# A hybrid attention layer on one core: the sample group's attention outputs in a bank of their own, and the value products ahead of the turn of q and k

## The chip, the core and the metric

The program runs on one core of one Trainium2 chip. The metric is device time in microseconds of one execution; the median of three runs counts. PE (TensorE) multiplies, DVE (VectorE), ACT (ScalarE) and POOL (GpSimd) work elementwise, and SP issues most of the DMA. Each engine works through a list of its own; semaphores order the lists against each other.

## The reference, cut to what matters

One layer of a hybrid decoder is computed for a prompt of 1024 tokens and for a sample group of 8 sequences with 8 new tokens each. Attention heads and a convolution stand side by side, their outputs go through one output projection, and a gated feed-forward block follows.

```python
z = rms_norm(x) @ w_in                        # q | k | v | a | gate
q, k = rms_norm(q), rms_norm(k)               # 8 heads of 64
attn = dilated windows (128,1), (512,4), (2048,16), combined by their softmax denominators
c = silu(layer_norm(causal_depthwise(a * sigmoid(gate), 31 taps)))
x = x + concat(attn, c) @ w_out
x = x + (silu(h @ w_gate) * (h @ w_up)) @ w_down,   h = rms_norm(x)
```

The prompt group attends to itself, the sample group to a cache of 1024 positions and its own new tokens. New cache rows and convolution states are outputs too. All products are made in float32 by three products of split operands (high times high, high times low, low times high: lines 330 to 332).

## The kernel before, in words

The stages are: the projections of the convolution branch (to about 140 us); q, k and v of the first pair of heads (to about 160 us); the attention loop (about 163 to 541 us); the rest of the output projection; the feed-forward block (about 600 us to the end), which is nothing but products for PE.

**The attention loop** has 40 steps: 4 pairs of heads (`p`), 10 steps each (`s`, in `STEPS`). Steps 0 and 5 are the sample group's two halves of 4 sequences ("s"), the other eight the prompt's query blocks of 128 tokens ("p", block `i`). `n = 10 p + s`. The order on each engine is written out by hand in one loop per engine; nothing schedules it. In step n:

- PE makes `scores(n + 1)` (products of q and k, lines 739, 743, 753), in pairs 0 to 2 the q, k and v columns of one token tile of the next pair (`qkv`, 24 products, lines 330 to 332, tile z, into bank 7), `turn_probs(n)` (transposes of the probabilities, lines 765, 774, into banks 4 and 5), `turn` (transposes of the q and k made one step earlier, lines 718, 720, into bank 7 too, so it must wait until ACT has emptied the tile just made: semaphore `z_ev`), and `values(n - 1)` (products of probabilities and values, lines 792 for the sample group, 808 and 815 for the prompt).
- DVE makes `mask_min` (mask and row minimum out of PSUM, line 1337), two or three `tap`s of the convolution (line 1249; each is one instruction over 1024 columns and one over the sample group's 64, both read SBUF twice), `normalise` (lines 1346, 1351), `square_sum` (lines 1312, 1315) and copies out the attention outputs: `block_outputs` (four prompt blocks of bank 6, line 1360), `scale_sample` (line 1389, into `so`) and `sample_outputs` (line 1360 over 64x32).
- ACT makes `exps` (line 1086), `keep` (empties the q, k, v tile: lines 1040, 1044, 1053), `copy_probs` (line 1095), `evict` (the turned q and k, lines 1079, 1081), and the high parts of the next weights (`high`, line 982).
- POOL makes the low parts of the weights (`low`, line 518, three per pair, around step 0) and the scaling of q and k (lines 534, 537, 543).

**The sample group's outputs** take a longer way. The products of step 0 or 5 are summed by `values`, scaled by DVE into `so`, turned back by PE (`turn_sample`, line 822) into the same bank, and copied out by DVE. Before, `sample_bank(p, half)` names the second score bank of the other parity: it is free from the end of `mask_min(n + 1)` until `scores` of the step after next. So PE makes these values early in steps 1 and 6 (before `qkv`), turns them at the end of the same step, and `scores` for steps 3 and 8, which PE issues in steps 2 and 7, wait for `d_se`, that is for `sample_outputs`, with which DVE begins steps 2 and 7. The prompt's outputs have bank 6.

In the last pair no q, k, v is left to make; there pieces of the output projection and of the convolution's layer norm (`fill`, `take_fill`) stand in three places of each step from step 3 on.

## Time and profile before

| | |
|---|---|
| median of three runs | 1425.53 us (1424.42 to 1427.17) |
| the profiled execution, its time | 1423.0 us |
| its span, first to last instruction | 1420.9 us |
| PE busy / PE weight loads busy | 93% / 88% of the span |
| DVE, ACT, POOL busy | 47%, 22%, 33% |
| mean granted clock of TensorE | 0.974 |
| chain that ended last | PE 82%, DVE 10%, issue 2%, ACT 2%, POOL 2% |

Times in the rows are in microseconds from the start of the span, durations of one instruction of a group in nanoseconds. In a timeline, a row is a run of like instructions: its start, its length, engine, line, operation, output and inputs, how many, and in brackets how long the engine sat idle before it and what ended that. Matmuls are pipelined, so the length of a run of them has a tail over which the next has already begun; the distance between two starts is the time that the first takes on PE. A TensorE clock of 1.0 is 2.4 GHz and 0.5 is 1.2 GHz.

### The profile page before, as it was taken

How to read it: one execution, taken by the hardware profiler on the slowest of the kernel's cores; microseconds unless marked ns; L12 is line 12 of the kernel's file. 1: busy time of each engine (PE TensorE's matmuls, PEld its weight loads, DVE VectorE, ACT ScalarE, POOL GpSimd, SP SyncE). 2: the span in 40 equal slices, each digit the busy share in tenths (PEclk: the TensorE clock that was granted, in tenths of full speed). 3: DMA queues.
4: the chain of work that ended last, by engine and by line, in shares of the span. 5: the costliest groups of instructions: out<-in, count | busy, mean ns of one | idle time of the engine just before them, and what ended most of it. 6: DMA issues, size and time to landing. Idle time of an engine off the chain costs nothing.

```text
span 1420.9 us, 22561 instructions
## 1 busy us (share of the span) xinstructions
PE 1317.1 (93%) x9084; PEld 1253.3 (88%) x9084; DVE 667.1 (47%) x1227; ACT 314.3 (22%) x715; POOL 474.0 (33%) x307
## 2 busy tenths in 40 slices
PE   6999789799795869999999999999999999999998
PEld 6999667677674559999999999999999999999998
DVE  6697867767678445583141414131313131313234
ACT  6212434444344325342101010101000000000000
POOL 0232522424215322533624242424242424333220
PEclk9999999999897879999999999999999999999999
DMA  7214143332435201038511410141114111411103
GB/s 223 64 53 145 31 150 101 111 104 77 138 104 213 83 18 43 31 119 282 194 44 60 149 60 31 52 157 46 45 45 163 44 47 35 171 33 60 38 0 126
DMA packets 50693, 131.07 MB, mean 92 GB/s; under 512 B 14480, under 2 KB 26640, under 8 KB 50064
## 3 DMA queue, kind: packets, MB, share of 16 engines
q1 hardware_dynamic: 45088, 95.47, 20.1%
q10 hardware_dynamic: 5504, 34.11, 7.1%
q8 instruction: 81, 1.33, 0.4%
q14 instruction: 20, 0.16, 0.0%
HBM read 120.09 MB, written 43.28 MB: 115 GB/s over the span
## 4 chain that ended last, share of the span: by engine, by line
PE 82%; DVE 10%; issue 2%; ACT 2%; POOL 2%; DMA 1%; SPq 0%; ACTq 0%; DVEq 0%; POOLq 0%
PE ps L330 25%; PE ps L332 25%; PE ps L331 25%; DVE uc L1249 5%; PE ps L743 1%; PE ps L808 1%; PE ps L739 1%; PE ps L815 1%; DVE ml_c L1494 1%; POOL zst L537 1%; PE ps L849 1%; PE ps L753 1%; DMA out_nk_p<-zst 1%; DVE tb L1337 1%; PE ps L718 1%
## 5 line engine op out<-in xcount | busy, mean ns | idle before, releaser
L637 POOL TENSOR_TENSOR wf<-raw,small 128x1024 fp32r<-128x1024 f32 x60 | 113.9, 1898 | 433.2 <-PE ps L332 423.4
L1573 DVE TENSOR_TENSOR pr<-ps,sg 128x362 f32<-128x362 f32 (+1 forms) x66 | 35.4, 536 | 411.0 <-ACT sg L1209 411.0
L330 PE MATMUL ps<-mh_a,wf 128*128 128x362 f32 (+1 forms) x624 | 207.7, 333 | 14.0 <-DVEq L1442 3.7
L1249 DVE SCALAR_TENSOR_TENSOR uc<-uc,small 128x1024 f32<-128x1024 f32 x240 | 215.1, 958 | 0.1
L332 PE MATMUL ps<-mh_a,wf 128*128 128x362 f32 (+1 forms) x624 | 205.5, 329 | 0.0
L331 PE MATMUL ps<-ml_a,wf 128*128 128x362 f32 (+1 forms) x624 | 205.4, 329 | 0.0
L331 PE MATMUL ps<-ml_c,wf 128*128 128x362 f32 (+1 forms) x624 | 203.9, 327 | 0.0
L332 PE MATMUL ps<-mh_c,wf 128*128 128x362 f32 (+1 forms) x624 | 203.9, 327 | 0.0
L330 PE MATMUL ps<-mh_c,wf 128*128 128x362 f32 (+1 forms) x624 | 203.5, 326 | 0.0
L1591 DVE TENSOR_TENSOR y<-ps,y 128x362 f32<-128x362 f32 (+1 forms) x264 | 139.4, 534 | 107.9 <-PE ps L332 107.9
L332 PE MATMUL ps<-ah,wf 128*128 128x364 f32 (+1 forms) x528 | 174.0, 330 | 0.0
L331 PE MATMUL ps<-al,wf 128*128 128x364 f32 (+1 forms) x528 | 173.7, 329 | 0.0
L330 PE MATMUL ps<-ah,wf 128*128 128x364 f32 (+1 forms) x528 | 173.4, 328 | 0.0
L1209 ACT ACTIVATE sg<-ps 128x362 f32<-128x362 f32 (+1 forms) x66 | 31.3, 474 | 620.7 <-PE ps L332 620.6
L639 POOL TENSOR_TENSOR wf<-raw,wf 128x1024 fp32r<-128x1024 f32 x60 | 147.5, 2458 | 4.7
L330 PEld LDWEIGHTS ps<-mh_a,wf 128*128 128x128 f32 x624 | 117.8, 189 | 18.3 <-DVEq L1442 4.3
L332 PEld LDWEIGHTS ps<-mh_a,wf 128*128 128x128 f32 x624 | 118.2, 189 | 0.0
L331 PEld LDWEIGHTS ps<-ml_a,wf 128*128 128x128 f32 x624 | 117.8, 189 | 0.2
L330 PEld LDWEIGHTS ps<-mh_c,wf 128*128 128x128 f32 x624 | 117.4, 188 | 0.0
L331 PEld LDWEIGHTS ps<-ml_c,wf 128*128 128x128 f32 x624 | 117.3, 188 | 0.0
L332 PEld LDWEIGHTS ps<-mh_c,wf 128*128 128x128 f32 x624 | 117.2, 188 | 0.0
L330 PE MATMUL ps<-wq,xh 128*128 128x384 f32 x288 | 103.4, 359 | 3.7 <-POOL wq L518 2.6
(150 smaller groups left out, 2118.7 us busy)
## 6 DMA issues: line engine op xcount, KB each, us to landing
raw<-in_w_stream SPq DMA_DIRECT2D x94, 512.0 KB, 3.5
skt<-in_kT_c SPq DMA_DIRECT2D x32, 384.0 KB, 5.3
sv<-in_v_c SPq DMA_DIRECT2D x32, 384.0 KB, 6.8
xr<-in_xT SPq DMA_DIRECT2D x8, 544.0 KB, 4.3
out_yT<-y SPq DMA_DIRECT2D x8, 544.0 KB, 2.7
y<-in_xT SPq DMA_DIRECT2D x1, 3264.0 KB, 15.3
out_nv_p<-vn SPq DMA_DIRECT2D x32, 64.0 KB, 1.8
out_nk_p<-zst SPq DMA_DIRECT2D x32, 64.0 KB, 1.6
```

What stands on the lines that cost most here:

```text
L330: e.matmul(out, wh, mh_, start=first, stop=False)
L331: e.matmul(out, wh, ml_, start=False, stop=False)
L332: return e.matmul(out, wl, mh_, start=False, stop=last)
L537: pool.tensor_tensor(rows, rows, r.unsqueeze(2).broadcast_to([P, 4, DH]), ALU.mult).then_inc(z_n, 1)
L637: pool.tensor_tensor(hi(m), src, zeros, ALU.add).then_inc(w_hi, 1)
L639: pool.tensor_tensor(lo(m), src, hi(m).bitcast(F32), ALU.subtract).then_inc(w_lo, 1)
L718: pe.transpose(turned(j), zst[:, z % 2, cols], ident[:]).then_inc(z_tr, 1)
L739: pe.matmul(ps[32 * r:32 * r + 32, (b + h) * 512:(b + h) * 512 + nf], q_[hr[h], i * P + 32 * r:i * P + 32 * r + 32], keys[:, r, :], start= ...
L1209: act.activation(sg[:, k6 % 2, 0:bn], bank(2 * (k6 % 2), bn), ACT.Silu).then_inc(gu_si, 1)
L1249: dve.scalar_tensor_tensor(out=dst, in0=src, scalar=w, in1=dst, op0=ALU.mult, op1=ALU.add).then_inc(s, 1)
L1573: dve.tensor_tensor(pr[:, k6 % 2, 0:bn], bank(2 * (k6 % 2) + 1, bn), sg[:, k6 % 2, 0:bn], ALU.mult).then_inc(gu_pr, 1)
L1591: dve.tensor_tensor(y[:, oc, b0:b0 + bn], bank(4 + m % 4, bn), y[:, oc, b0:b0 + bn], ALU.add).then_inc(dn_y, 1)
```

## The change

Three things change. The sample group's outputs move to columns 0 to 127 of bank 6, which they share in time with the prompt's: `values` of a sample step waits until the prompt's last four blocks are copied out (`d_oe`), `values` of blocks 0 and 4 until the sample group's are (`d_se`), and the waits on `d_tt` in the sample's `values` and on `d_se` in `scores` go. Its transposition back moves from the end of steps 1 and 6 to steps 2 and 7, after the scores and before `qkv`; `scale_sample` moves to the start of steps 2 and 7 on DVE, `sample_outputs` behind `mask_min`, and `block_outputs` ahead of it. In every step PE makes `values(n - 1)` before `turn`, and in steps 1 and 6 after `qkv` instead of before it. The reciprocal of the sample's denominators gets a column of its own (`rden_s`), since it is read one step later.

```diff
--- before.py
+++ after.py
@@ -160,6 +160,7 @@
         rs8 = small[:, 59:68]
         mns, den, rden = small[:, 68:72], small[:, 72:76], small[:, 76:80]
         ssz = small[:, 80:84]
+        rden_s = small[:, 209:210]
 
         def place(at, name, shape, dt=F32):
 
@@ -251,9 +252,8 @@
 
             return bank(7, w, j * P)
 
-        def sample_bank(p, half):
-
-            return bank(2 * ((NSTEP * p + 5 * half + 1) % 2) + 1, P)
+
+        sample_bank = bank(6, P)
 
         g_in, c_in = sem("gain_in"), sem("consts_in")
         x_in = [sem(f"x_in{k}") for k in range(KT)]
@@ -728,8 +728,6 @@
                 q_, k_ = qt[p % 2], kt_[p % 2]
                 if kind == "p":
                     pe.wait_ge(t_ev, 2 * (NT * p + i + 2))
-                    if s in (3, 8):
-                        pe.wait_ge(d_se, 2 * p + s // 5 + 1)
                     nf = far(i)
                     k0 = max(i - 1, 0) * P
                     hr = [slice(DH * h, DH * h + DH) for h in range(2)]
@@ -780,9 +778,10 @@
                 kind, i = STEPS[s]
                 pe.wait_ge(d_ev, 2 * n + 2)
                 if kind == "s":
-                    pe.wait_ge(d_tt, ROWS0[n + 2])
+                    if 2 * p + i:
+                        pe.wait_ge(d_oe, 2 * p + i)
                     r = slice(64 + NEW * i, 64 + NEW * (i + 1))
-                    out = sample_bank(p, i)
+                    out = sample_bank
                     for c in range(CKT + 1):
                         for bb in range(4):
                             if c == 0:
@@ -795,7 +794,7 @@
                     last.then_inc(d_pv, 1)
                     return
                 if i % 4 == 0:
-                    pe.wait_ge(d_oe, 2 * p + i // 4)
+                    pe.wait_ge(d_se, 2 * p + i // 4 + 1)
                 if i == 2:
                     pe.wait_ge(d_vf, 32 * (p + 1))
                 first = max(i - 1, 0)
@@ -819,7 +818,7 @@
 
             def turn_sample(p, half):
                 pe.wait_ge(d_so, 2 * p + half + 1)
-                pe.transpose(sample_bank(p, half), so[:], ident[:]).then_inc(d_ot, 1)
+                pe.transpose(sample_bank, so[:], ident[:]).then_inc(d_ot, 1)
 
             def project(out, ks, oc, g):
                 b0, bn = BLOCKS[g]
@@ -873,21 +872,19 @@
                 fills = p == NPAIR - 1 and s in FILL
                 if n + 1 < NALL:
                     scores(n + 1)
-                if s in (1, 6):
-                    values(n - 1)
+                if s in (2, 7):
+                    turn_sample(p, s // 5)
                 if z_at(p, s) is not None:
                     qkv(z_at(p, s))
                 if fills:
                     fill(s, 0)
                 turn_probs(n)
-                if s in (1, 6):
-                    turn_sample(p, s // 5)
+                if fills:
+                    fill(s, 1)
+                if n >= 1:
+                    values(n - 1)
                 if turn_at(p, s) is not None:
                     turn(turn_at(p, s))
-                if fills:
-                    fill(s, 1)
-                if n >= 1 and s not in (1, 6):
-                    values(n - 1)
                 if fills:
                     fill(s, 2)
             values(NALL - 1)
@@ -1343,7 +1340,7 @@
                 dve.wait_ge(d_ex, ROWS0[n + 1])
                 r = 2 * (n % 2)
                 k = len(heads(n))
-                dve.reciprocal(rden[:, r:r + k], den[:, r:r + k]).then_inc(d_rc, 1)
+                dve.reciprocal(rden_s if k == 1 else rden[:, r:r + k], den[:, r:r + k]).then_inc(d_rc, 1)
                 if k == 1:
                     return
                 dve.wait_ge(d_rc, n + 1)
@@ -1386,11 +1383,11 @@
                 n = NSTEP * p + 5 * half
                 dve.wait_ge(d_pv, n + 1)
                 dve.wait_ge(d_rc, n + 1)
-                dve.tensor_scalar(so[:], sample_bank(p, half), col(rden, n, 0), None, ALU.mult).then_inc(d_so, 1)
+                dve.tensor_scalar(so[:], sample_bank, rden_s, None, ALU.mult).then_inc(d_so, 1)
 
             def sample_outputs(p, half):
                 dve.wait_ge(d_ot, 2 * p + half + 1)
-                o = sample_bank(p, half).rearrange("p (b c) -> p b c", c=32)
+                o = sample_bank.rearrange("p (b c) -> p b c", c=32)
                 c0 = SEQ + NEW * half
 
                 def part(a, r):
@@ -1462,15 +1459,15 @@
                 p, s = divmod(n, NSTEP)
                 fills = p == NPAIR - 1 and s in FILL
                 if s in (2, 7):
-                    sample_outputs(p, s // 5)
-                if n + 1 < NALL:
-                    mask_min(n + 1)
-                if s in (1, 6):
                     scale_sample(p, s // 5)
                 if s == 6:
                     block_outputs(2 * p)
                 if s == 1 and p >= 1:
                     block_outputs(2 * p - 1)
+                if n + 1 < NALL:
+                    mask_min(n + 1)
+                if s in (2, 7):
+                    sample_outputs(p, s // 5)
                 if s == 5 and p < NPAIR - 1:
                     fill_qb(p + 1)
                 for _ in range(TAPS_STEP.get(n, 0)):
```

**How the lists of instructions move.** First PE, step 3 of the first pair, from the second head's transposed probabilities on (`tb` probabilities, `zst` q and k before the turn, `pt` turned probabilities, `vn` values). Before:

```order
L774 MATMUL ps<-ident,tb 128x128 [waits probs_out,normed]
L774 MATMUL ps<-ident,tb 128x128
L774 MATMUL ps<-ident,tb 32x128
L718 MATMUL ps<-ident,zst 128x128 [waits qkv_evicted,qk_turned_out,qkv_normed]
L718 MATMUL ps<-ident,zst 128x128
L808 MATMUL ps<-pt,vn0 64x128 [waits probs_out]
L808 MATMUL ps<-pt,vn0 64x128 x3
L753 MATMUL ps<-skt,qb 32x512 [waits qb_ready,sample_k_in0,qk_turned_out,scores_masked]
```

Changed:

```order
L772 MATMUL ps<-ident,tb 128x128 [waits probs_out,normed]
L772 MATMUL ps<-ident,tb 128x128
L772 MATMUL ps<-ident,tb 32x128
L807 MATMUL ps<-pt,vn0 64x128 [waits probs_out]
L807 MATMUL ps<-pt,vn0 64x128 x3
L718 MATMUL ps<-ident,zst 128x128 [waits qkv_evicted,qk_turned_out,qkv_normed]
L718 MATMUL ps<-ident,zst 128x128
L751 MATMUL ps<-skt,qb 32x512 [waits qb_ready,sample_k_in0,qk_turned_out,scores_masked]
```

The two transposes of q and k with their waits stand behind the value products instead of ahead of them; no row is added.

Second, PE, from the end of `turn_probs` of step 6 of the first pair to the scores of step 7 (`so` the scaled sample outputs). Before:

```order
L774 MATMUL ps<-ident,tb 128x128 [waits probs_out,normed]
L774 MATMUL ps<-ident,tb 128x128
L774 MATMUL ps<-ident,tb 96x128
L822 MATMUL ps<-ident,so 128x128 [waits sample_scaled]
L718 MATMUL ps<-ident,zst 128x128 [waits qkv_evicted,qk_turned_out,qkv_normed]
L718 MATMUL ps<-ident,zst 128x128
L739 MATMUL ps<-kt0,qt0 32x160 [waits sample_out,qk_turned_out,scores_masked]
L739 MATMUL ps<-kt0,qt0 32x160 x7
L743 MATMUL ps<-kt0,qt0 128x256 x2
```

Changed (from the middle of the sample's value products, which now stand here, to the transposition back):

```order
L791 MATMUL ps<-sv,pt 32x128 [waits sample_v_in3]
L791 MATMUL ps<-sv,pt 32x128 x20
L791 MATMUL ps<-vfar,pt 32x128 x4
L718 MATMUL ps<-ident,zst 128x128 [waits qkv_evicted,qk_turned_out,qkv_normed]
L718 MATMUL ps<-ident,zst 128x128
L737 MATMUL ps<-kt0,qt0 32x160 [waits qk_turned_out,scores_masked]
L737 MATMUL ps<-kt0,qt0 32x160 x7
L741 MATMUL ps<-kt0,qt0 128x256 x2
L821 MATMUL ps<-ident,so 128x128 [waits sample_scaled]
```

The wait on `sample_out` at the scores is gone; the transposition back, with its wait on `sample_scaled`, now stands behind them, with the next tile's `qkv` right behind it.

Third, DVE, from the masks of step 1 of the second pair to those of step 2 (`mkp` mask; ISA is the masking instruction). Before:

```order
L1337 ISA small 128x1
L1389 TENSOR_SCALAR so<-ps,small 128x128 [waits den_recip,values_summed]
L1360 COPY ao<-ps 128x4x4x32 [waits values_summed]
L1249 SCALAR_TENSOR_TENSOR uc<-uc,small 128x1024 [waits conv_prompt]
L1249 SCALAR_TENSOR_TENSOR uc<-uc,small 128x8x8 [waits conv_samples]
...
L1315 TENSOR_SCALAR small<-small 128x4 [waits qkv_square_sums]
L1360 COPY ao<-ps 64x32 [waits sample_turned]
L1360 COPY ao<-ps 64x32
L1337 ISA tb,small<-ps,mkp 128x288 [waits probs_turned,scores]
```

Changed:

```order
L1348 TENSOR_SCALAR tb<-tb,small 128x128
L1357 COPY ao<-ps 128x4x4x32 [waits values_summed]
L1334 ISA tb,small<-ps,mkp 128x256 [waits probs_turned,scores]
...
L1312 TENSOR_SCALAR small<-small 128x4 [waits qkv_square_sums]
L1386 TENSOR_SCALAR so<-ps,small 128x128 [waits den_recip,values_summed]
L1334 ISA tb,small<-ps,mkp 128x288 [waits probs_turned,scores]
L1334 ISA small 128x1
L1334 ISA tb,small<-ps,mkp 128x288
L1334 ISA small 128x1
L1357 COPY ao<-ps 64x32 [waits sample_turned]
```

The big copy out of bank 6 now comes ahead of the step's masks, the scaling has moved past three taps, the normalising and the squares to the start of step 2, and the two small copies behind the masks of step 2.

## Rows read from the trace of the kernel before

**Rows 1.** The page's 40 slices: busy tenths of PE.

```profile
PE   6999789799795869999999999999999999999998
```

**Rows 2.** Waits of PE, 165 to 545 us: sum, times, longest.

```profile
PE ps L739 <- DVE ao L1360: 19.4, 5, 6.2
PE ps L718 <- ACT vn L1053: 11.1, 21, 0.6
PE ps L739 <- DVE ml_a L1368: 8.4, 2, 6.9
...
PE ps L720 <- ACT vn L1053: 2.5, 3, 0.8
```

**Rows 3.** Timeline of PE, first pair, steps 2 and 4.

```profile
193.76 0.31 PE L720 MATMUL ps<-ident,zst 64*128 64x64 f32 x2 [0.84 <-ACT vn L1053]
...
207.77 0.82 PE L774 MATMUL ps<-ident,tb 128*128 128x128 f32 x6
209.22 0.41 PE L718 MATMUL ps<-ident,zst 128*128 128x128 f32 x2 [0.62 <-ACT vn L1053]
209.55 0.66 PE L808 MATMUL ps<-pt,vn 128*64 128x128 f32 x8
210.14 0.65 PE L815 MATMUL ps<-pt,vfar 32*64 32x32 f32 x16
210.73 0.55 PE L739 MATMUL ps<-kt,qt 64*32 64x96 f32 x16
```

**Rows 4.** Timeline of ACT, step 4 of the first pair.

```profile
209.96 0.39 ACT L1081 ACTIVATE kt<-ps,small 128x128 f32<-128x128 f32 x1
```

**Rows 5.** Timeline of PE, steps 6 and 7, first pair; last row second pair.

```profile
219.05 0.66 PE L739 MATMUL ps<-kt,qt 64*32 64x128 f32 x16
...
220.28 1.52 PE L792 MATMUL ps<-sv,pt 128*32 128x128 f32 x48
...
226.35 0.82 PE L774 MATMUL ps<-ident,tb 128*128 128x128 f32 x6
227.00 0.27 PE L822 MATMUL ps<-ident,so 128*128 128x128 f32 x1
...
229.01 0.78 PE L739 MATMUL ps<-kt,qt 64*32 64x160 f32 x16 [0.81 <-ACT kt L1081]
...
317.53 0.79 PE L739 MATMUL ps<-kt,qt 64*32 64x160 f32 x16 [1.25 <-DVE ao L1360]
```

**Rows 6.** Windows of qkv: stretch, length, PE busy (count), granted clock, DMA share, GB/s.

```profile
318.98:324.69 5.71, 5.71 (x26) 0.72 0.08 23
364.85:371.44 6.59, 6.59 (x27) 0.61 0.00 0
...
230.42:234.62 4.20, 4.20 (x25) 1.00 0.10 31
```

**Rows 7.** Timeline of PE, step 9 of the first pair: the turn, next scores.

```profile
253.16 0.41 PE L718 MATMUL ps<-ident,zst 128*128 128x128 f32 x2 [0.40 <-ACT vn L1053]
...
255.11 0.49 PE L743 MATMUL ps<-kt,qt 64*128 64x128 f32 x4
```

**Rows 8.** Timeline of all engines, step 0 of the second pair.

```profile
258.90 2.39 DVE L1249 SCALAR_TENSOR_TENSOR uc<-uc,small 128x64 f32<-128x64 f32 x1
...
261.59 3.35 POOL L518 TENSOR_TENSOR wq<-raw,wq 128x1024 fp32r<-128x1024 f32 x1
```

**Rows 9.** Timeline of DVE, second pair, the end of the work before step 2's masks.

```profile
272.79 0.38 DVE L1360 COPY ao<-ps 64x32 f32<-64x32 f32 x2
```

**Rows 10.** Timeline of PE, step 2 of the second pair.

```profile
273.32 0.36 PE L739 MATMUL ps<-kt,qt 64*32 64x32 f32 x16 [6.16 <-DVE ao L1360]
...
274.77 0.69 PE L330 MATMUL ps<-wq,xh 128*128 128x384 f32 x1
```

**Rows 11.** Timeline of PE, last pair, steps 7 and 8.

```profile
510.01 0.80 PE L739 MATMUL ps<-kt,qt 64*32 64x160 f32 x16 [1.44 <-DVE ml_a L1368]
...
521.30 1.29 PE L853 MATMUL ps<-ones_c,sq 128*128 128x1 f32 x6 [3.40 <-POOL sq L584]
```

## The prediction

> **What bounds the kernel now.** I read the page first. PE is busy in nine tenths of nearly every slice; the gaps are in slices 4 to 16, the attention loop [rows 1]. After it nothing but products follows, and the change does not touch them. So I asked for PE's waits between 165 and 545 us. Two kinds can be touched by the change: scores of steps 2 and 7 that wait for the copy of the sample group's outputs (19.4 + 8.4 = 27.8 us in 7 waits, up to 6.9 us each), and the turn of q and k, which waits for ACT to empty the tile just made (11.1 + 2.5 = 13.6 us in 24 waits) [rows 2]. The timelines of PE, ACT, DVE and POOL around single steps then show what would end each wait next. The reader should see in them that PE sets the pace of steps 2 to 9, while DVE and POOL set it at steps 0 and 1.
>
> **Term 1, the turn behind the value products.** In step 4, PE's transposed probabilities start at 207.77 and take 0.65 (226.35 to 227.00, the same six of them [rows 5]), so PE is free at 208.42; the turn starts at 209.22, takes 0.33, and the value products take 1.18 (209.55 to 210.73) [rows 3]. In the new order the value products run from 208.42 to 209.60, the emptying is over by then, and the turn follows at once: the step is 0.80 shorter. In step 2 the value products last only some 0.37, less than the wait of 0.84 [rows 3], so 0.36 is saved and the rest of the wait stays. By the same working steps 3, 5, 7 and 8 save 0.59, 0.65, 0.79 and 0.58. That is 3.8 a pair, in three pairs **11.3**. From below, the listed idle times alone would give 3.2 a pair, 9.5. What could take the gain back is the next `qkv`, which waits for the turned q and k to be evicted: they were evicted 1.13 after the start of the turn (209.22 to 209.96 + 0.39) [rows 3, 4]. The turn takes 0.33 and the first part of the scores 0.55 [rows 3], the second part comes on top, so the eviction stays hidden, with little room. I cost it at nothing; without that cover a step would lose about half a microsecond.
>
> **Term 2, steps 6 and 7.** From the scores issued in step 6 (219.05) to the q, k, v products of step 7 (230.42, a window's start) were 11.37 [rows 5, 6]. In the new order this path is: scores 1.23 (to 220.28); value products of the sample group and q, k, v products together 6.07 (220.28 to 226.35, in either order); transposes 0.65; turn 0.33; scores 1.41 (229.01 to 230.42); transposition back 0.20. Sum 9.9, gain 1.5. In the two other pairs the scores waited 1.25 instead of 0.81 [rows 5], so about 1.9 each. Together **5.4**. The new wait in it is that of the transposition back for the scaling. DVE had finished the work of step 6 just before 229.01, the sample copies of 0.38 included, and the wait for the sample's products in the middle of it (0.8) goes; so the scaled outputs lie ready near 227.6, a microsecond before PE asks. Nothing is queued too late behind it.
>
> **Term 3, the clock after that wait.** In the second pair the 24 products of step 7 took 5.71 at a granted clock of 0.72, in the first pair 4.20 at 1.00 [rows 6]. Without the wait ahead of them I take the full clock: **1.5**. From below nothing.
>
> **Term 4, steps 0 to 2 of each pair.** Here DVE is late. POOL's three splits of the next weights stand around step 0, and DVE's taps and they shut each other out: the tap over 64 columns took 2.39 and ended with the split beside it [rows 8]. After the third split (261.59 + 3.35 = 264.94) DVE worked without a stop until 273.17 (272.79 + 0.38) [rows 8, 9]; only then came the scores at 273.32, and the q, k, v products at 274.77 [rows 10]. In the new order the scores (1.45) are made meanwhile, and the small copies (0.38) come later; the transposition back (0.20) stands between the scaling and the q, k, v products. That is 1.6 earlier. But the splits start later: in step 9 the turn moves behind the value products of 1.6 (253.16 to 255.11, less 0.33) [rows 7], thus from 253.16 to 254.26; ACT evicts it and only then makes the high parts that the splits need. ACT's queue was 0.35 late anyhow, so 0.75 remains. Net 0.85 at the second and third pair, 1.6 at the first, where no step 9 comes before, and in the last, where the small copies are four instructions and POOL splits the mixed outputs as well, I take 1.0: with **4.4** in all. The sample's value products (1.8), which in step 1 move behind the q, k, v products, cost nothing as long as DVE is later still: they end near 269, the scaling near 273.5. From above, all of the 0.75 would be hidden and 6.4 gained; from below nothing.
>
> On the port, the Trainium skill (SBUF — State Buffer, section "SBUF: two separate sides") says that whichever of DVE and GpSimd starts first holds the shared ports for its whole instruction and that the other blocks fully. The trace agrees with the blocking (2.39 for 64 columns). By that rule the first tap of step 0, which now starts before the first split, would hold the split up by what is left of it, and term 4 would be some 0.8 smaller over the pairs.
>
> **Term 5, the last pair's second half.** The scores of step 7 waited 1.44 for the sample copies [rows 11], and the value products of 1.8 stood ahead of the layer norm's pieces, with DVE waiting for them. After those scores the chain runs over the masks, the exponentials, ACT's high part, POOL's split and POOL's sums of squares to the products at 521.30, which waited 3.40 for POOL [rows 11]. So what the scores gain is passed on. Between nothing and 1.44 + 1.8 = 3.2 I take **2.3**, since the block copy and the pieces of the layer norm keep DVE busy for the rest.
>
> The sum is 11.3 + 5.4 + 1.5 + 4.4 + 2.3 = 24.9. Against the profiled execution's 1423.0 that is 1398.1; the median of the runs is 2.5 higher, so the forecast for the median is **1400.6**.
>
> **The rivals.**
>
> *A, the clock comes back at the pairs' starts too.* PE's gap in steps 1 and 2 shrinks from 6.16 [rows 10] to some 3.5, broken by value products and scores. After the long gap the third pair's products of step 2 took 6.59 at 0.61, against 4.20 at 1.00 [rows 6]. If they ran at the full clock, up to 2.4 more would be won there, and near 4.7 over three pairs: 1396. Against it stands that a short gap was enough to lower the clock to 0.72 in Term 3, and that the products of step 1 wait for weights before it. The Trainium skill (TensorE: Matmul & The Clock Gate, "What's actually happening") calls the low clock the default state, which activity lifts; by that rule a denser PE would come out nearer to this case. Chance 0.14.
>
> *B, the eviction is the next wait.* ACT's queue is keep, probabilities, eviction; if the eviction comes late in most steps, q, k, v products wait for it and Term 1 is given back. The room is only the second part of the scores [rows 3, 4]. The time would be 1400.6 + 11.3 = 1412. Chance 0.08.
>
> *C, the sample wait only moves.* The transposition back now stands ahead of q, k and v. If DVE brought the scaling as late as it brought the copies, Terms 2 to 5 would shrink to the scores' own length or less; with Term 1 alone left, 1414. For it: at the pairs' starts it does move so. Against it: in the second halves DVE has the microsecond of Term 2. Chance 0.08.
>
> *D, slower: the splits slide into step 1.* Should the third split come more than 2 us later than before, it would meet the three taps of step 1 instead of DVE's PSUM work, and each of the six tap instructions can be shut out; three stalls of 2.39 [rows 8] at three pair starts cost 21.5, and the longer gaps keep the low clock for all of step 2's products, up to 2.4 each [rows 6], 7.2 in all. Term 4 goes, and 28.7 stands against the 20.5 that is left: 8 slower, 1434. I work out 0.75 and not 2, so the chance is 0.02.
>
> That the change does not do what it says I hold for unlikely: the lists show the rows moved and no wait added besides those named.
>
> **How the numbers follow.** The forecast has 0.62, A 0.14, B 0.08, C 0.08, D 0.02; 0.06 lies between forecast and no change. The range of 8 in 10 reaches from A with a little (1395) to the sum of the lower bounds, 9.5 + 5.4 = 14.9 without Terms 3 to 5, which is 1410.6: 1395 to 1410. Under 0.2% (2.9 us) a measurement of this kernel can't tell from no change. Faster by more: forecast, A, B, C and most of the rest, 0.95; within it 0.03; slower 0.02.
>
> **What would show it.** In the changed profile the turn should wait only in step 2 (about 0.5) and hardly elsewhere; the scores of steps 2 and 7 should wait for nothing; the transposition back should wait some 3 us at three or four pair starts and not in the second halves; step 7's products of the second pair should take 4.2; the stretch after the loop should be as long as before. The prediction is wrong if `qkv` waits for ACT in most steps, if the transposition back waits in steps 7, or if taps in step 1 run beside a split.

## The result and the profile after

The changed kernel takes **1392.26 us** (median of 4 runs, 1389.53 to 1395.79) against 1425.11 of the kernel before: ratio 0.9769, 95% interval 0.9738 to 0.9799. The direction is as forecast. The size is not: 1392.3 lies below the forecast of 1400.6 and below the low end of the range, 1395. The profiled execution took 1394.82, its span 1392.9, at a mean granted clock of 0.975 (before 0.974).

The page's slices of the changed kernel answer to [rows 1]; PEclk is the granted clock in tenths.

```profile
PE   6999799899995799999999999999999999999998
...
PEclk9999899899997989999999999999999999999999
```

In slices 6, 11 and 15, which had 8, 7 and 6, PE is now at 9; the start of the loop (slice 5), that of the second pair (slice 8, now 8) and that of the last pair (slices 13 and 14) are left. The list of PE's waits, 160 to 545 us of the changed kernel, answers to [rows 2] (sum, times, longest):

```profile
PE ps L821 <- DVE so L1386: 8.9, 4, 2.8
PE ps L772 <- DVE tb L1348: 8.5, 2, 6.6
...
PE ps L330 <- ACT kt L1078: 3.6, 2, 1.8
...
PE ps L720 <- ACT vn L1050: 1.4, 3, 0.5
```

Of the 27.8 us at the scores nothing is left, and of the turn's 13.6 us only the three waits of 0.5 in step 2. The new wait is that of the transposition back (L821), at the four pair starts alone. The timeline of PE, first pair, steps 4 and 6 to 7, answers to [rows 3, 5]:

```profile
205.89 0.82 PE L772 MATMUL ps<-ident,tb 128*128 128x128 f32 x6
206.64 0.66 PE L807 MATMUL ps<-pt,vn 128*64 128x128 f32 x8
207.23 0.65 PE L814 MATMUL ps<-pt,vfar 32*64 32x32 f32 x16
207.81 0.44 PE L718 MATMUL ps<-ident,zst 128*128 128x128 f32 x2
208.18 0.55 PE L737 MATMUL ps<-kt,qt 64*32 64x96 f32 x16
...
215.97 0.66 PE L737 MATMUL ps<-kt,qt 64*32 64x128 f32 x16
...
224.38 0.78 PE L737 MATMUL ps<-kt,qt 64*32 64x160 f32 x16
...
225.72 0.33 PE L821 MATMUL ps<-ident,so 128*128 128x128 f32 x1
```

No row has a bracket: value products, turn, scores and transposition back follow each other without a wait. From step 6's scores to step 7's q, k, v products (a window's start, 225.80) are 9.83 us; the prediction worked out 9.9.

To see where the time went I cut the attention loop at four kinds of points of PE's timeline: start of step 2's q, k, v products, end of step 9's, first product of the layer norm, end of the loop.

| stretch, in us | before | after | less |
|---|---|---|---|
| loop's start to step 2's products, first pair | 27.06 | 25.30 | 1.76 |
| step 9's end to step 2's products, second / third pair | 23.05 / 23.06 | 21.23 / 21.17 | 1.82 / 1.89 |
| step 9's end to the first layer norm product, last pair | 31.99 | 30.25 | 1.74 |
| step 2's 24 products, three pairs | 5.08, 5.63, 6.59 | 4.24, 6.97, 4.24 | 1.85 |
| from their end to step 9's end, three pairs | 59.40, 61.39, 59.86 | 54.66, 54.67, 54.67 | 16.65 |
| from there to the loop's end, last pair | 78.56 | 74.70 | 3.86 |
| loop | 381.67 | 352.10 | 29.57 |

The loop began 1.67 later in this execution (161.85 against 160.18), ahead of anything that the change touches, and what follows it is as long as before (879.05 against 878.95 us).

### The profile page after: what moved, and what is told of

The parts are those of the page before. It is cut to its first block, busy times and chain, and to the rows that moved or that the text cites. A ratio compares the mean times of both kernels' runs of the same rounds, so it can differ in the third digit from the quotient of the medians.

```text
span 1392.9 us, 22561 instructions
## 1 busy us (share of the span) xinstructions
PE 1319.2 (95%) x9084; PEld 1255.7 (90%) x9084; DVE 669.7 (48%) x1227; ACT 316.7 (23%) x715; POOL 473.1 (34%) x307
## 4 chain that ended last, share of the span: by engine, by line
PE 85%; DVE 9%; issue 2%; POOL 2%; DMA 1%; ACT 1%; SPq 0%; ACTq 0%; DVEq 0%; POOLq 0%
PE ps L330 26%; PE ps L332 25%; PE ps L331 25%; DVE uc L1246 4%; PE ps L772 1%; PE ps L807 1%; PE ps L814 1%; PE ps L741 1%; DVE ml_c L1491 1%; POOL zst L537 1%; PE ps L848 1%; PE ps L751 1%; PE ps L737 1%; DMA out_nk_p<-zst 1%; DVE tb L1334 1%
## 5 line engine op out<-in xcount | busy, mean ns | idle before, releaser
L1246 DVE SCALAR_TENSOR_TENSOR uc<-uc,small 128x1024 f32<-128x1024 f32 x240 | 210.7, 940 | 0.3
```

The source lines that it names most:

```text
L1246: dve.scalar_tensor_tensor(out=dst, in0=src, scalar=w, in1=dst, op0=ALU.mult, op1=ALU.add).then_inc(s, 1)
```

## The experiments

**The same kernel again.** No edit, six more executions.

> The changed kernel once more, unaltered. Its four runs fell into two pairs, 1394.8 and 1395.8, and 1389.7 and 1389.5, with mean granted clocks of 0.975 and 0.979; the profiled one was of the first kind, and in it the q, k, v products of step 2 of the second pair took 6.97 us at a clock of 0.57, those of the first and third pair 4.24 at 1.00. Clock theory: the two kinds differ in which products run at 1.2 GHz and in nothing else; more runs will lie at about 1389.6 or about 1395, and if the profile is of the faster kind, the products of step 2 take about 4.2 in all three pairs. Rival (the kinds differ in waits, as in how DVE and POOL come to share their port): the products' times are alike and the waits of PE differ by 5 us.

1395.13 us (median of 6, 1392.28 to 1404.36), ratio 0.9797, 0.9774 to 0.9820. The six do not gather at 1389.6 and 1395, and the profiled one (1392.28) is of neither kind. All ten executions of the changed kernel have the median 1394.7. The windows of step 2's products in this trace (stretch, length, busy time of PE, PEld, DVE, ACT and POOL, granted clock, DMA share, GB/s), and the turn back ahead of each:

```profile
185.66:189.90 4.24, 4.24 (x26) 4.21 (x26) 4.16 (x12) 1.15 (x4) 1.30 (x2) 1.00 0.67 234
265.71:271.52 5.81, 5.81 (x25) 5.78 (x26) 4.71 (x13) 1.15 (x4) 1.29 (x2) 0.71 0.69 225
347.37:353.18 5.81, 5.81 (x26) 5.78 (x27) 4.72 (x13) 1.15 (x4) 1.29 (x2) 0.71 0.48 171
```

```profile
185.56 0.33 PE L821 MATMUL ps<-ident,so 128*128 128x128 f32 x1 [2.32 <-DVE so L1386]
...
265.62 0.33 PE L821 MATMUL ps<-ident,so 128*128 128x128 f32 x1 [1.25 <-DVE so L1386]
...
347.27 0.33 PE L821 MATMUL ps<-ident,so 128*128 128x128 f32 x1 [2.21 <-DVE so L1386]
```

The same 24 products took 4.24, 5.81 and 5.81 here and 4.24, 6.97 and 4.24 above. The length of the wait does not decide it: 2.8 us was followed by either clock in one and the same execution, and 1.2 by either in the two. Every other stretch agrees within 0.5 us, except that step 1's products ran at other speeds (5.33, 6.89 and 7.04 us against 6.43, 6.45 and 6.42), and the wait behind them was longer or shorter by about as much. The two loops are equally long (352.11 and 352.10 us), so the 2.7 us between the two spans lie outside the loop: 1.5 ahead of it and 1.2 behind it. The two say nothing for or against the clock theory.

**The order alone.** The kernel before, with values ahead of the turn:

```diff
-                if turn_at(p, s) is not None:
-                    turn(turn_at(p, s))
                 if fills:
                     fill(s, 1)
                 if n >= 1 and s not in (1, 6):
                     values(n - 1)
+                if turn_at(p, s) is not None:
+                    turn(turn_at(p, s))
```

> The kernel before, with only the value products put ahead of the turn of q and k (in steps other than 1 and 6, where they already are). Terms as measured in the changed trace: about 3.3 us a pair from steps 2, 3, 4, 5, 7, 8 and 0.4 from step 9, in all 11, and perhaps 1.5 where the clock no longer falls in step 7. Forecast 1412 to 1415 against 1425.1. If the turn's place mattered for the pair starts as well (POOL's splits later, taps first), the waits of the scores of steps 2 shrink or grow by up to 1 us each. If the parts only work together, it is above 1418.

1412.42 us (1411.35 to 1414.59), ratio 0.9905, 0.9890 to 0.9919. From step 2's products to step 9's end, those products left out, it saves 3.27, 3.28 and 3.28 us: Term 1 by itself, 3.3 a pair and not 3.8. The waits for ACT at the turn (L718) are gone from its list, those at the scores stand:

```profile
PE ps L739 <- DVE ao L1360: 17.2, 5, 5.8
PE ps L739 <- DVE ml_a L1368: 8.4, 2, 6.9
```

**The bank alone.** The changed kernel with the turn ahead of the values again (the same edit backwards).

> The changed kernel, with the turn put back ahead of the value products in every step: the sample group's bank, its turn one step later and the order on DVE stay. Additive theory: it gives back the 11 us of the reordering and keeps the rest: 1403 to 1406. Rival (the bank is worth little, since the wait only moves to the scaling): 1412 or more. In steps 7 no wait of the scores on DVE; in steps 2 a wait for the scaling of 1 to 3 us.

1409.01 us (1404.91 to 1412.32), ratio 0.9883, 0.9865 to 0.9902: a few us above what I had expected. In its trace all three of step 2's products had the low clock (5.81, 5.80, 5.81), and the turn's waits are back (L718, 11.4 us in 21). The pair starts are as short as in the changed kernel (25.30, 21.31, 21.33 us), so nearly the whole of Term 4 belongs to the bank (the order alone has 26.46, 22.91 and 22.88, that is 0.6, 0.1 and 0.2 less than before). Between the pair starts it saves 0.8, 2.8 and 1.3 us. With the 3.3 of the order that leaves 0.6 of each pair to the two together, since in step 6 the value products now stand between the emptying and the turn. The medians fit: the order alone saves 12.9, the bank alone 16.3, both together 30.7 by the ten executions.

**The turn's place in step 9.** The changed kernel, but in step 9 alone the turn ahead of the values:

```diff
+                if s == 9 and turn_at(p, s) is not None:
+                    turn(turn_at(p, s))
                 if fills:
                     fill(s, 1)
                 if n >= 1:
                     values(n - 1)
-                if turn_at(p, s) is not None:
+                if s != 9 and turn_at(p, s) is not None:
```

> The changed kernel, with the turn ahead of the value products in step 9 alone, so that ACT can make the high parts of the weights as early as before. My step in term 4: the splits on POOL start 0.75 later because of the turn; undone, the three pair starts would win 0.75 each, less the 0.4 that step 9 loses: about 1 us faster in all. Rival, from the changed trace: the third split ended only 0.26 us later than before, since the first tap now runs ahead of the first split and POOL waits for one tap less; then the turn's place costs nothing there and this kernel is 1 to 2 us slower.

1395.18 us (1390.67 to 1402.49), ratio 0.9795, 0.9768 to 0.9822. The pair starts took 21.31 us, against 21.23 and 21.17. Turning earlier brings nothing, so the 0.75 us that I took off Term 4 for it does not exist. Where it went is seen in the timeline of DVE and POOL, second pair, changed kernel:

```profile
249.96 7.32 DVE L1246 SCALAR_TENSOR_TENSOR uc<-uc,small 128x1024 f32<-128x1024 f32 x4
250.75 5.05 POOL L518 TENSOR_TENSOR wq<-raw,wq 128x1024 fp32r<-128x1024 f32 x2 [1.15 <-ACT wq L979]
...
257.16 2.37 POOL L518 TENSOR_TENSOR wq<-raw,wq 128x1024 fp32r<-128x1024 f32 x1
...
257.39 2.42 DVE L1348 TENSOR_SCALAR tb<-tb,small 128x128 f32<-128x128 f32 x2
259.73 1.06 DVE L1357 COPY ao<-ps 128x512 f32<-128x512 f32 x1
```

```profile
246.05 1.03 PE L772 MATMUL ps<-ident,tb 128*128 128x128 f32 x8
...
248.63 0.44 PE L718 MATMUL ps<-ident,zst 128*128 128x128 f32 x2
```

The turn does come later, 2.58 after the transposes of step 9 (246.05 to 248.63) against 1.44 (251.72 to 253.16 in the trace before): the 1.1 that was worked out. But the third split ended 13.48 after those transposes (259.53) against 13.22 before (264.94 less 251.72), so only 0.26 later. The first tap now comes before the first split; the two taps with what shuts them out took 7.32 instead of 8.95, and the taps were over (257.28) when the third split had hardly begun (257.16), where before the last of them stood shut out until that split had ended [rows 8, 9]. So DVE's two normalising instructions, 0.48 us by themselves, now stand beside the third split (2.42) and no longer behind it. With the turn early in step 9 the order of before comes back: the first split begins at 249.52, ahead of the first tap (250.06), the taps take 8.93, and though the third split ends 13.19 after the transposes instead of 13.48, DVE begins its block copy 13.78 after them instead of 13.68. Of the splits' late start nothing reached DVE's end.

**The turn back behind q, k and v.** Would the last wait go? The changed kernel with `turn_sample` behind `qkv` on PE and `sample_outputs` behind the taps on DVE:

```diff
-                if s in (2, 7):
-                    turn_sample(p, s // 5)
                 if z_at(p, s) is not None:
                     qkv(z_at(p, s))
+                if s in (2, 7):
+                    turn_sample(p, s // 5)
```

> The changed kernel, with the sample's transposition back behind the q, k, v products of steps 2 and 7, and the small copies on DVE behind the taps. PE then has nothing to wait for before those products. If the wait for the scaling (8.9 us in 4 waits in the changed trace) is what is left of the old one, it goes: 6 to 9 us faster than the changed kernel, and the products after it come at the full clock more often. Rival (DVE sets the pace at the pair starts, whatever PE waits on): the scores of step 3 or the transposes of step 2 wait in its place and less than 3 us is won.

1394.37 us (1387.91 to 1399.13), ratio 0.9751, 0.9712 to 0.9790: nothing gained where 6 to 9 us were expected. Timeline of PE in the second pair, and the windows of the products of steps 2 and 3:

```profile
265.29 0.27 PE L821 MATMUL ps<-ident,so 128*128 128x128 f32 x1
...
268.22 0.69 PE L807 MATMUL ps<-pt,vn 128*64 128x128 f32 x4 [2.22 <-DVE ao L1357]
```

```profile
261.03:265.29 4.26, 4.26 (x26) 4.23 (x25) 4.19 (x13) 1.01 (x4) 1.52 (x2) 1.00 1.05 336
270.79:276.97 6.18, 6.18 (x26) 6.15 (x25) 5.85 (x13) 1.20 (x4) 0.89 (x2) 0.66 0.58 192
```

The pair starts are 3 us shorter (18.20 and 18.19), but the value products of block 0, which take bank 6 over, wait 2.2 for the copies (2.5 in the third pair), and behind this wait the clock is low in step 3 (6.18 and 6.06 where the changed kernel has 4.28; in the first pair, where the wait is 0.40, it is 4.27). The wait changes its place and takes the low clock along. Over the three pairs that comes out even. The profiled execution, the slowest of the four, loses another 7.5 us in the last pair, 4.1 of them by step 6's scores, where a split on POOL met DVE's normalising (Term 5 below). Whether that is the edit's doing one trace can't show.

**PE kept busy in the wait.** Ahead of `turn_sample` in step 2, twelve more products of 128x384 into the bank of q, k and v:

```diff
+                if s == 2 and z_at(p, s) is not None:
+                    pe.wait_ge(z_ev, z_at(p, s))
+                    for _ in range(12):
+                        pe.matmul(zbank, xh[:, 0, 0:P], wq[:, 0, 0:384], start=True, stop=True)
                 if s in (2, 7):
                     turn_sample(p, s // 5)
```

> The changed kernel, with 12 products more than the computation needs (384 columns each, into bank 7, overwritten by the q, k, v products that follow) ahead of the transposition back in step 2 of the first three pairs, where PE waits for DVE. They add nothing to the path where the wait is over 2.1 us (at 2.4 GHz), and about 1 us at the first pair, whose wait is 1.2. Clock theory: the products behind them take 4.2 us in all three pairs instead of 4.2 to 7.0, so the runs gather at the low end, about 1390 to 1392, with less spread. Rival (the clock there is set by what came further back, in step 1): the products still take 5.8 in some pairs, and the kernel is 0 to 2 us slower than the changed one.

1391.61 us (1388.46 to 1394.71), ratio 0.9746, 0.9712 to 0.9779. Windows of the needed products of step 2, and the turn back of the second pair:

```profile
187.73:191.97 4.24, 4.24 (x26) 4.20 (x25) 3.88 (x9) 0.32 (x2) 0.30 (x1) 1.00 0.79 277
267.82:272.06 4.24, 4.24 (x26) 4.21 (x27) 4.16 (x12) 1.15 (x4) 1.28 (x2) 1.00 0.65 246
347.93:352.17 4.24, 4.24 (x26) 4.21 (x26) 4.16 (x12) 1.15 (x4) 1.28 (x2) 1.00 0.69 252
```

```profile
267.72 0.33 PE L821 MATMUL ps<-ident,so 128*128 128x128 f32 x1 [0.54 <-DVE so L1390]
```

The added 2.35 us of products a pair cost nothing where DVE is waited for long enough (from step 1's to step 2's products 12.43 and 12.45 in the second and third pair, against 12.47 and 12.41 in the changed kernel) and 1.1 in the first pair (11.91 against 10.84), and all three stretches behind them ran at 1.00. Step 1's products were as slow as ever (6.68, 6.44 and 7.03), so the rival that it is they that set the clock of step 2 fell. The median is 3.1 below that of the ten executions. That fits (ten of fifteen at the low clock, 1.6 or more each, is some 3.2 for three pairs), but the runs overlap and their spread is no smaller than that of the first four (both 6.3 us), so the trace carries this reading and not the median.

**The block copy's place.** The changed kernel with `block_outputs` behind `mask_min` again, as before the change.

> The changed kernel, with only the order of two pieces on DVE put back: the copy of the prompt's four blocks behind the masks of steps 1 and 6 instead of ahead of them. The sample's value products wait for that copy. I expect next to nothing in the first three pairs (under 0.5 us each way), since at those steps PE makes q, k and v first, which covers 0.7 us; in the last pair's step 6 the multiplies of the layer norm come no earlier either. Within 1.5 us of the changed kernel. If the copy's place were part of why the pair starts gained more than I forecast, e9 to step 2 would be over 21.7 us instead of 21.2.

1395.72 us (1392.56 to 1399.06), ratio 0.9783, 0.9752 to 0.9815. The pair starts are 25.29, 21.17 and 21.17 us, the same to a tenth: at the pair starts this part of the change is worth nothing either way. In the last pair's step 6 it is worth something, against the expectation: PE waits 4.01 us instead of 3.24 for the multiplies of the layer norm, and step 7's scores come 0.6 later than in the trace of the turn in step 9, whose last pair is otherwise the same (45.00 against 44.36 after the first layer norm product). Step 2's products took 4.24, 4.24 and 5.81.

**Taps away from the pair starts.** If DVE is late there because of its taps, they should stand elsewhere. The same 24 a pair:

```diff
-TAPS_STEP = {n: 3 if n % NSTEP in (1, 3, 6, 8) else 2 for n in range((NPAIR - 1) * NSTEP)} | {30: 2, 31: 2, 32: 2}
+TAPS_STEP = {n: (1, 2, 2, 3, 3, 3, 3, 2, 3, 2)[n % NSTEP] for n in range((NPAIR - 1) * NSTEP)} | {30: 2, 31: 2, 32: 2}
```

> The changed kernel, with one tap fewer in each of steps 0 and 1 and one more in steps 3 to 5, 6 as before, so that DVE has 2.8 us less to do where PE waits for it. If the pair starts are bound by DVE's list behind POOL's third split, the wait for the scaling shrinks by about 1.4 us a pair (the tap of step 1; that of step 0 is hidden beside the splits anyhow), and PE's steps 2 to 9 hide the taps: 3 to 6 us faster in all. Rival (steps 3 to 5 have become bound by DVE since the reordering shortened them): the gain is given back there and the kernel is within 2 us or slower.

**1382.17 us** (1377.60 to 1382.22), ratio 0.9670, 0.9638 to 0.9702, faster than both kernels. Timelines of PE and DVE, second pair, and the window of step 2's products:

```profile
262.01 0.33 PE L821 MATMUL ps<-ident,so 128*128 128x128 f32 x1
```

```profile
261.25 0.35 DVE L1386 TENSOR_SCALAR so<-ps,small 128x128 f32<-128x128 f32 x1
```

```profile
262.09:266.35 4.26, 4.26 (x26) 4.23 (x27) 4.14 (x12) 1.15 (x4) 0.74 (x2) 1.00 1.04 305
```

The scaled outputs are there 0.4 before PE turns them back. The pair starts fell from 21.2 to 17.4 us, that is the wait of 2.8 and, with step 1's products at 5.5 instead of 6.4, another 0.9. Steps 3 to 9, which took the taps in, are as long as before to a hundredth (54.67, 54.66, 54.66 us).

**Further, once more, in the last pair, and in the old kernel.** The last four ran side by side on one chip; each is described in its expectation.

> The changed kernel with the taps of pairs 0 to 2 shared out as (0,1,2,3,3,3,3,3,3,3) over steps 0 to 9, one less in steps 0 and 1 than where they were (1,2,2,3,3,3,3,2,3,2). Theory (DVE's lateness at the pair starts is what the kernel pays for, and with (1,2,2,...) it is already paid off in pairs 0 to 2: PE had no wait for DVE there from 170 to 400 us): no further gain, 1380 to 1384 us, from the step-9 products to the step-2 products 17.3 as before. Rival one (the low clock in steps 0 and 1 comes from splits that DVE holds up): the splits end some 1 us earlier, 3 us in all, 1378. Rival two (three taps in seven steps are too many for DVE): waits of the transposes for `tb` appear in steps 5 to 9 and the time rises to 1386 or more.

1380.22 us (1379.08 to 1383.92), ratio 0.9677, 0.9651 to 0.9703: no further gain, as the first theory had it. Pair starts 17.38 and 16.98.

> The kernel with taps (1,2,2,3,3,3,3,2,3,2) once more, so that it stands beside the two above on one chip: 1379 to 1384 us. By the theory of the clock (a wait of 2.8 us ahead of step 2's products lowers it in some executions, none where there is no wait) the products of step 2 take 4.24 to 4.3 us in all of pairs 0 to 2 again. If the full clock in the first profile of it was luck, one or more of the three takes 5.8 or more.

1380.52 us (1379.04 to 1382.73), ratio 0.9679, 0.9655 to 0.9704. Step 2's products 4.24, 4.25 and 4.25. So the full clock was not luck.

> The changed kernel with 25 taps in each of pairs 0 to 2, as (1,2,2,3,3,3,3,3,3,2), and 0, 1 and 2 instead of 2, 2 and 2 at the start of the last pair. Theory (DVE's lateness again: in the last pair the transposes waited 6.6 and 2.0 us for the normalised probabilities, the turn back 2.7 and the first layer norm products 2.9 for the taps): most of these 14 us goes, against 1382 us I expect 1370 to 1375. Rival (POOL's splits and ACT set the start of the last pair, so that the waits only change their name): 1379 to 1383.

**1373.58 us** (1369.96 to 1376.36), ratio 0.9623, 0.9598 to 0.9649, the best of all, 6.9 below the kernel with the taps moved in three pairs. Timeline of PE at the start of the last pair, first that kernel, then this one:

```profile
407.36 0.48 PE L772 MATMUL ps<-ident,tb 128*128 128x128 f32 x1 [6.58 <-DVE tb L1348]
409.82 0.48 PE L772 MATMUL ps<-ident,tb 128*128 128x128 f32 x1 [1.99 <-DVE tb L1348]
...
417.44 0.47 PE L821 MATMUL ps<-ident,so 128*128 128x128 f32 x1 [1.79 <-DVE so L1386]
```

```profile
402.68 0.30 PE L772 MATMUL ps<-ident,tb 128*128 128x128 f32 x1 [0.94 <-ACT pt L1092]
404.28 0.47 PE L772 MATMUL ps<-ident,tb 128*128 128x128 f32 x1 [1.31 <-DVE tb L1348]
...
413.51 0.47 PE L821 MATMUL ps<-ident,so 128*128 128x128 f32 x1 [3.38 <-DVE so L1386]
```

The transposes' 8.6 us shrank to 2.3, the turn back gave 1.6 of it back. From step 9's end to the first layer norm product it is 4.9 less. The profiled execution of this kernel was the slowest of its six; what the medians show beyond 4.9 I can't place.

> The kernel before, with nothing changed but the taps: (1,2,2,3,3,3,3,2,3,2) over steps 0 to 9 of pairs 0 to 2. If the gain of moving taps and the gain of the change are independent (the change shortens what stands behind DVE at a pair start, the taps make DVE less late), the time falls as far as it did in the changed kernel, 12 to 13 us: 1411 to 1415, and the idle time of PE ahead of step 2's scores from 6.2 to about 2. If instead what holds those scores is the length of the way values, scaling, turn back, copies and not DVE's lateness, the gap stays over 4 and the time falls by less than 6: 1419 or more.

1414.86 us (1413.23 to 1417.62), ratio 0.9921, 0.9895 to 0.9947. The time is that of the first theory, the gap is that of the second: PE's timeline in the second pair has

```profile
267.33 0.36 PE L739 MATMUL ps<-kt,qt 64*32 64x32 f32 x16 [4.18 <-DVE ao L1360]
```

so 4.2 us are left of 6.2 [rows 10], and step 2's products behind it still took 6.15 and 5.78 us (4.26 in the first pair, behind a wait of 1.28). Moving taps saves 2.9 us at the second and third pair start in the old order and 3.85 in the new one, so the two gains are not independent there. In the old order the scores still wait for copies that stand behind step 1's taps and its normalising on DVE.

## Why the prediction was right or wrong

**What bounds the kernel**, and what would show it: right in all five points, but for one length. The turn waits in step 2 alone (0.5), the scores of steps 2 and 7 wait for nothing, the transposition back waits at four pair starts (1.2 to 2.8, not "some 3") and in no second half, step 7's products of the second pair took 4.25, and the stretch after the loop is as long as before.

**Term 1** (11.3) was mis-sized a little: alone it measured 9.8, 3.28 a pair. What was too low is the 0.65 for the six transposes. I took it from a place where a transposition back followed [rows 5]; with value products behind them they held PE for 0.75 (205.89 to 206.64), and the turn with scores behind it 0.37 instead of 0.33. The rest is as worked out: the eviction stayed hidden, `qkv` waits for ACT (L1078) only in step 1, so rival B fell.

**Terms 2 and 3** (5.4 and 1.5): right, but for a slip (1.5 + 1.9 + 1.9 is 5.3). With Term 1 they came to 16.65, so 6.8 for the two together; of it 0.6 a pair needs both parts of the change.

**Term 4** (4.4) is **the step that failed**. It measured 7.2: 1.76, 1.82, 1.89 and 1.74 at the four pair starts. (Its own parts, 0.85 twice, 1.6 and 1.0, are 4.3.) The 1.6 worked out from the scores, the copies and the turn back was right in the first pair. What was wrong was "0.75 remains" for the later splits, at the second and third pair. The prediction passed a delay of POOL's start on to DVE's end as if the two worked in a chain. They take turns instead, and which comes first changes what each is shut out by: the third split ended 0.26 later, and DVE did its normalising beside it instead of behind it. Turning early in step 9 put the old order of the two back and brought nothing (21.31 against 21.2). "From above, all of the 0.75 would be hidden and 6.4 gained" was the case that came. Why the last pair gave 1.74 and not the 1.0 taken for it, no run shows.

By the Trainium skill (SBUF — State Buffer, section "SBUF: two separate sides") of a DVE instruction with two SBUF inputs and a GpSimd instruction the one that starts first keeps the shared ports for its whole length. I had drawn from it that Term 4 would be smaller. The trace agrees with the blocking (two taps took 7.32 us beside the splits and 2.87 in step 9), not with that inference: an earlier tap cost the splits 0.26 us and spared DVE more.

**Term 5** (2.3) was too small: 3.9 in this trace. Step 7's scores came 3.9 earlier after the first layer norm product (42.81 against 46.72 us):

```profile
482.06 0.79 PE L737 MATMUL ps<-kt,qt 64*32 64x160 f32 x16
...
492.77 0.78 PE L852 MATMUL ps<-ones_c,sq 128*128 128x1 f32 x6 [1.02 <-POOL sq L584]
```

That looks like the whole of 1.44 + 1.8, but 1.5 of it was there before the sample group had a part in it, at step 6's scores (31.40 against 32.88 us). Of that 0.3 is how fast the first layer norm products ran (7.22 against 7.56 to the next products), and 1.2 is a wait of PE for DVE in step 3 that is gone. Timelines of DVE, POOL and PE there, before:

```profile
471.07 2.80 DVE L1351 TENSOR_SCALAR tb<-tb,small 128x320 f32<-128x320 f32 x2
471.21 4.90 POOL L518 TENSOR_TENSOR wf<-raw,wf 128x1024 fp32r<-128x1024 f32 x2 [8.16 <-ACT wf L982]
...
474.37 0.43 PE L330 MATMUL ps<-mh_a,wf 128*128 128x362 f32 x1 [1.16 <-DVE y L1412]
```

and changed:

```profile
446.70 0.68 DVE L1348 TENSOR_SCALAR tb<-tb,small 128x320 f32<-128x320 f32 x2
448.62 4.71 POOL L518 TENSOR_TENSOR wf<-raw,wf 128x1024 fp32r<-128x1024 f32 x2 [9.60 <-ACT wf L979]
```

In the trace before, the split begins while DVE normalises, and in the changed one it begins later. Whether they meet changes from one execution to the next: the two traces of the kernel with the taps moved have 0.68 and 2.81, and the stretch from the first layer norm product to the loop's end took 72.67 and 74.62 us in them. The trace of the turn in step 9, whose last pair is that of the changed kernel, has 2.81 as the one before. In it the scores of step 7 come 2.4 earlier (44.36), near the 2.3, of which 0.6 is the block copy's place; and from there to the loop's end 1.2 more is gained (30.59 against 31.84), which the prediction put at nothing when it took what the scores gain as simply passed on. In all that is 3.6 (74.95 against 78.56).

**Rival A, the clock at the pair starts,** came in part. The gap fell to 2.8, and to 1.2 in the first pair, not to 3.5. In five traces with this wait (the changed kernel twice, the bank alone, the turn in step 9, the block copy's place) the products behind it ran at full clock 5 times in 15 and took 5.80 to 6.97 the other ten. In the five traces where PE had at most a third of a microsecond to wait there (turn back late, taps moved twice, further, last pair) it was 15 of 15 at 4.24 to 4.28, and 3 of 3 with PE kept busy. So the wait causes the low clock, but not each time. The forecast had put these products at nothing; in the profiled execution they gave 1.9 (17.30 to 15.45 us for the three). That this is also part of why executions differ (the changed kernel spread from 1389.5 to 1404.4, the one with the taps moved from 1377.6 to 1382.7) is likely, but no two traces show it. I had given the two outcomes as one or the other, where each pair start draws anew. Rivals C and D fell: no wait came up in the second halves, and in the second pair's trace no split stood beside step 1's taps.

**The sum.** The loop gave 29.6 where 24.9 was forecast: 1.5 less by Term 1, 0.1 less by Terms 2 and 3, 2.8 more by Term 4, 1.6 more by Term 5, 1.9 more by the clock of rival A. Against the profiled executions' own times the change was 28.2 (1423.0 to 1394.8), since the loop started 1.7 later. That is 3.3 of the miss of 8.3. The other 5 us lie between profile and median: I took the median 2.5 above the profiled execution, and it was 2.6 below. That part is luck of the draw: by the median of all ten executions, 1394.7, the result is 0.3 outside the range and not 2.7.

## What to carry to other kernels

Where two engines shut each other out, a late start of one is not a late end of the other; place the blocks in turn before passing a delay on. And when a change removes waits, ask who sets the pace at the place that is left: here it was DVE's taps at the pair starts, and moving a few of them to steps with room won 12 to 14 us more for a table of ten numbers, some 21 with the last pair's (against the ten executions' 1394.7). The wait itself could not be moved: put behind q, k and v, it came back at the next value products, with the low clock behind it.

## What was not expected of the hardware

- Behind a wait of PE of 1.2 to 2.8 us the same 24 products ran at a granted clock of 1.00 (4.24 us), 0.71 (5.81) or 0.57 (6.97), and the wait's length did not tell which; behind the three waits of 3.2 they took 5.80 or 5.81. With twelve products inside the wait it was 1.00 in three of three. The Trainium skill (TensorE: Matmul & The Clock Gate, "What's actually happening") says that activity releases the throttle. These traces agree, and add that the outcome differs between executions of one kernel.
- Behind a wait of 2.2 us, with value products, turn and scores in between, the q, k, v products that followed ran at 0.66 (6.18 us instead of 4.28), although the products ahead of the wait had run at 1.00.
- The normalising was shut out by a split too: in step 3 of the last pair its two instructions of 320 columns took 0.68 us alone and 2.80 where a split ran beside them, and which of the two it is differs between executions of one kernel (0.68 and 2.81).
- One row of a matmul group does not give its price in another place: six transposes held PE for 0.65 ahead of a transposition and for 0.75 ahead of value products.
